# Output projection of a decoder layer in seven half-block products, residual and last bias by accumulating DMAs

## The chip, the core and the metric

The kernel runs on one core of one Trainium2 chip. The metric is the device time in microseconds of one execution, the median of three runs. The core has a matrix engine (TensorE, PE in the profile), VectorE (DVE), ScalarE (ACT), GpSimd (POOL) and SyncE (SP), each with its own instruction stream. SP and POOL issue the DMAs, each into its own queue. The engines meet only through semaphores.

## What is computed

One layer over 2048 tokens and 1024 channels, in float32. The part that the change touches is the last two lines: the output projection, the gated residual and the LayerNorm.

```python
h = x * (1.0 + scale) + shift
proj = h @ w_in[layer] + b_in[layer]
...
merged = jax.nn.sigmoid(g_mix_a) * y_attn + jax.nn.sigmoid(g_mix_b) * y_conv
sub = gate * (merged @ w_out[layer] + b_out[layer])
x = _layer_norm(DEEPNORM_ALPHA * x + sub, ln_g[layer], ln_b[layer])
```

The LayerNorm takes mean and variance over the 1024 channels of each token, then multiplies by `ln_g` and adds `ln_b`.

## The kernel before

Every large product is made in three passes of a rounded type: each operand is split into a high part (ScalarE copies it into the rounded type) and a low part (VectorE subtracts the high part from the original). The passes are high by high, high by low and low by high. So one product of a 128 x 512 result over 128 channels costs three matmuls of 512 columns.

**Input projection (68 groups).** A group computes a 2 x 2 block of results, two tiles of 128 outputs by two halves of 512 tokens, over two halves of the channels. It does this with seven products in place of eight (`NP = 7`): `combine` makes the sums and differences of the weight blocks on VectorE, `round_w` (ScalarE) and `split_w` (VectorE) make high and low parts, `product` issues 12 matmuls. The products are numbered n = 7 * group + p, and all five engines run the same loop over m, this number: ScalarE rounds the weights of product m + 4, VectorE splits those of m + 3 and takes the results of product m - 1, TensorE runs product n once its parts are there and its PSUM bank is free. Product p = 6 starts only when VectorE has taken p = 4 of its group (`pe.wait_ge(c22_out, g + 1)`).

**SP's queue in that loop.** `load_w(g)` fetches the weights of a group. `load_mix(u, dg)` fetches attention results, in nine DMAs for a unit u. The first unit is loaded at m = 448 to 450 and consumed by VectorE's `mix` at m = 452, 453, 454 (`MIX_AT`), after the taking and splitting of the same step. SP runs ahead of the other engines and stands only at its semaphore waits, so all nine DMAs leave right behind `load_w(65)`.

**Attention and conv projections (32 units n).** `project_att(n)` and `project_conv(n)` make a 128 x 512 tile. `gate_att` and `merge` on VectorE weigh both with their gates, and POOL's `store_m` writes the merged tile to `mix_d`. The gate-weighted output weights lie in `wos_d` since the middle of the kernel. During the last eight units SP loads them (`load_wo`), ScalarE rounds and VectorE splits them.

**Output projection (16 tiles tt of 128 tokens).** `load_m` fetches the merged rows of a tile, `round_m` and `split_m` make its parts, and TensorE runs 2 halves x 8 channel blocks x 3 passes = 48 matmuls for each tile, with the tokens as the stationary operand. `load_xr` fetches the residual rows. VectorE makes alpha * x + gate * bias, adds the product, takes mean and variance with `bn_stats`, and after ScalarE's normalization multiplies by `ln_g` and adds `ln_b`. POOL stores the tile. The last tile (`LAST`) is added and measured in two halves and stored in two halves.

## Time and profile before

| | us |
|---|---|
| median of 3 runs | 1870.26 (1868.84 to 1872.65) |
| the profiled execution, own time | 1868.47 |
| its span in the trace | 1866.7 |
| TensorE busy in the span | 1849.8 |
| VectorE busy | 1214.1 |
| ScalarE busy | 840.7 |

The page gives for each engine its busy time, its share of the span and its number of instructions. In a timeline each row is a start, a duration, an engine, a line, the operation with its tiles, a count, and in brackets how long the engine stood before it and for whom. DMA rows give the size of one and the median time from issue to landing. A matmul row's duration overlaps the next one's, so the pace is read from starts.

### The profile page before, as it was taken

How to read it: one execution, taken by the hardware profiler on the slowest of the kernel's cores; microseconds unless marked ns; L12 is line 12 of the kernel's file. 1: busy time of each engine (PE TensorE's matmuls, PEld its weight loads, DVE VectorE, ACT ScalarE, POOL GpSimd, SP SyncE). 2: the span in 40 equal slices, each digit the busy share in tenths (PEclk: the TensorE clock that was granted, in tenths of full speed). 3: DMA queues.
4: the chain of work that ended last, by engine and by line, in shares of the span. 5: the costliest groups of instructions: out<-in, count | busy, mean ns of one | idle time of the engine just before them, and what ended most of it. 6: DMA issues, size and time to landing. Idle time of an engine off the chain costs nothing.

```text
span 1866.7 us, 24546 instructions
## 1 busy us (share of the span) xinstructions
PE 1849.8 (99%) x8879; PEld 1508.0 (81%) x8879; DVE 1214.1 (65%) x2086; ACT 840.7 (45%) x1493; POOL 183.0 (10%) x305
## 2 busy tenths in 40 slices
PE   8999999999999999999999999999999999999998
PEld 7788888888888888878878888888888888888886
DVE  8755744456666666675686766666657576646776
ACT  5644633445545555666674545555454310012221
POOL 0223011100000000111210000000111100000000
PEclk9999999999999999999999999999999999999999
DMA  9866523332322222455853222222354988784442
GB/s 372 296 234 242 200 111 113 98 128 72 111 88 95 86 95 82 153 190 180 296 212 101 94 80 91 82 88 87 113 176 135 287 238 225 219 276 135 147 136 101
DMA packets 156648, 292.38 MB, mean 157 GB/s; under 512 B 35344, under 2 KB 87312, under 8 KB 152816
## 3 DMA queue, kind: packets, MB, share of 16 engines
q1 hardware_dynamic: 131056, 202.87, 33.9%
q0 software_dynamic: 25184, 87.35, 12.7%
q8 instruction: 72, 1.18, 0.3%
q10 hardware_dynamic: 288, 0.59, 0.1%
q14 instruction: 48, 0.39, 0.1%
HBM read 202.37 MB, written 88.38 MB: 156 GB/s over the span
## 4 chain that ended last, share of the span: by engine, by line
PE 95%; DVE 2%; ACT 1%; DMA 1%; issue 1%; ACTq 0%; POOL 0%; DVEq 0%
PE acc L1120 22%; PE acc L1125 21%; PE acc L1128 21%; PE acc L1329 3%; PE acc L1278 3%; PE acc L1282 3%; PE acc L1321 3%; PE acc L1325 3%; PE acc L1274 3%; PE score L1185 2%; PE xb L1218 2%; PE acc L1136 1%; PE xb L1201 1%; PE pt_o L1201 1%; DMA vt_d<-room 1%
## 5 line engine op out<-in xcount | busy, mean ns | idle before, releaser
L1120 PE MATMUL acc<-t_hi,w_hi 128*128 128x512 f32 x1848 | 509.2, 397 | 3.0 <-DVE room L1625 1.8
L1125 PE MATMUL acc<-t_lo,w_hi 128*128 128x512 f32 x1848 | 495.0, 390 | 0.0
L1128 PE MATMUL acc<-t_hi,w_lo 128*128 128x512 f32 x1848 | 494.9, 390 | 0.0
L1125 PEld LDWEIGHTS acc<-t_lo,w_hi 128*128 128x128 f32 x1848 | 346.9, 188 | 74.1
L1128 PEld LDWEIGHTS acc<-t_hi,w_lo 128*128 128x128 f32 x1848 | 346.9, 188 | 73.8
L1120 PEld LDWEIGHTS acc<-t_hi,w_hi 128*128 128x128 f32 x1848 | 337.1, 188 | 82.2 <-issue 13.1
L1625 DVE TENSOR_TENSOR room<-acc,part 128x512 f32<-128x512 f32 x198 | 136.8, 691 | 219.7 <-PE acc L1128 213.9
L1421 ACT ACTIVATE part<-acc,cols 128x512 f32<-128x512 f32 x198 | 136.8, 691 | 209.8 <-PE acc L1128 209.4
L1625 DVE TENSOR_TENSOR room<-room 128x512 f32<-128x512 f32 (+3 forms) x223 | 176.5, 795 | 73.8 <-ACT room L1451 30.7
L1625 DVE TENSOR_TENSOR w_lo<-w_raw,w_hi 128x512 fp32r<-128x512 f32 x272 | 183.7, 687 | 40.8 <-ACT w_hi L1404 39.2
L1404 ACT CAST w_hi<-w_raw 128x512 fp32r<-128x512 f32 x264 | 162.8, 617 | 90.2 <-PE acc L1128 87.6
L1404 ACT CAST w_hi<-s_tmp 128x512 fp32r<-128x512 f32 x198 | 122.9, 621 | 164.5 <-PE acc L1128 147.3
L1625 DVE TENSOR_TENSOR w_lo<-s_tmp,w_hi 128x512 fp32r<-128x512 f32 x198 | 136.2, 688 | 69.2 <-ACT w_hi L1404 66.5
L1486 ACT ACTIVATE room<-room 128x128 f32<-128x128 f32 (+1 forms) x192 | 86.9, 454 | 54.7 <-DVE room L1871 54.5
L1001 POOL DMA_DIRECT2D att_d<-room x48 | 34.5, 718 | 530.1 <-DVE room L1878 530.1
L1625 DVE TENSOR_TENSOR w_raw<-w_raw 128x512 f32<-128x512 f32 x98 | 67.5, 689 | 4.9
L1867 DVE CUSTOM_DVE_ANT_0 room<-score,room 128x128 f32<-128x128 f32 (+1 forms) x192 | 58.7, 362 | 16.6 <-PE score L1185 16.3
L1625 DVE TENSOR_TENSOR w_raw<-acc,w_raw 128x512 f32<-128x512 f32 x32 | 22.1, 690 | 68.1 <-PE acc L1282 68.1
L1625 DVE TENSOR_TENSOR s_tmp<-w_raw,s_tmp 128x512 f32<-128x512 f32 x66 | 45.6, 690 | 29.4 <-PE acc L1128 26.3
L1505 ACT CAST t_hi<-t_raw 128x2048 fp32r<-128x2048 f32 x6 | 11.5, 1917 | 116.6 <-DMA t_raw<-conv_d 116.6
L1321 PE MATMUL acc<-t_hi 128*128 128x512 f32 x256 | 63.2, 389 | 0.0
L1329 PE MATMUL acc<-t_hi,t_lo 128*128 128x512 f32 x256 | 63.2, 389 | 0.0
(224 smaller groups left out, 2067.8 us busy)
## 6 DMA issues: line engine op xcount, KB each, us to landing
w_raw<-in_w_tiles SPq DMA_DIRECT2D x132, 512.0 KB, 4.5
gate_d<-room POOLq DMA_DIRECT2D x64, 256.0 KB, 3.8
w_raw<-gate_d SPq DMA_DIRECT2D x32, 512.0 KB, 5.6
qk_d<-room POOLq DMA_DIRECT2D x24, 512.0 KB, 5.1
room<-qk_d SPq DMA_DIRECT2D x74, 128.0 KB, 3.6
t_raw<-tr_d SPq DMA_DIRECT2D x8, 1024.0 KB, 7.1
conv_d<-room POOLq DMA_DIRECT2D x16, 512.0 KB, 3.0
mix_d<-w_raw POOLq DMA_DIRECT2D x32, 256.0 KB, 5.6
```

The lines of the kernel that those rows point to most:

```text
L1120: nc.tensor.matmul(to, w_hi[:, s, k], t_hi[:, p, k], start=(first and k == 0), stop=False, skip_group_check=True)
L1125: nc.tensor.matmul(to, w_hi[:, s, k], t_lo[:, p, k], start=False, stop=False, skip_group_check=True)
L1128: mm = nc.tensor.matmul(to, w_lo[:, s, k], t_hi[:, p, k], start=False, stop=(last and k == KH - 1), skip_group_check=True)
L1274: nc.tensor.matmul(to, w_h[:, k], b_half(True, k), start=(k == 0), stop=False)
L1278: nc.tensor.matmul(to, w_l[:, k], b_half(True, k), start=False, stop=False)
L1321: nc.tensor.matmul(to, m_h[:, k], wo_hi[:, k, w], start=(k == 0), stop=False)
L1329: mm = nc.tensor.matmul(to, m_l[:, k], wo_hi[:, k, w], start=False, stop=(k == KT - 1))
L1404: nc.scalar.copy(w_hi[:, n % RING], src).then_inc(hi_done, 1)
L1421: ins = nc.scalar.activation(to, src, ACT.Identity, bias=col(gr.tb if p == 1 else gr.ta))
L1486: ex = nc.scalar.activation(prob[:, h, o], prob[:, h, o], ACT.Exp, bias=all_m[:, t, h, b], scale=SCALE, accum_out=all_d[:, t, h, b])
L1625: return nc.vector.tensor_tensor(o, a, b, op)
L1867: own_t.up(nc.vector.tensor_tensor_reduce(out=prob[:, h, o], in0=sc_ps[:, h, o], in1=bm[:, h, o.start - 2 * P * s:2 * P], scale=1.0, scala ...
```

## The change

The output projection gets the seven-product scheme of the input projection. Its 16 tiles become 8 blocks (`NO`) of 256 tokens. A block is two token tiles by two halves of 512 outputs over two halves of the channels. The loop numbers go on past the 476 products of the input projection (`NS`) to 532 (`NALL`). `product`, `round_w`, `split_w` and `combine` serve both: the stationary operand is the merged tokens, which `load_m(h)` now puts into `w_raw`, and the moving one is the output weights.

- Three of the four combinations of the output weights and one block more come from a new DRAM tensor `to_d`. It is made during the input projection in four rounds (`WQ_AT` = 425, 431, 437, 443): SP loads 1 MB of `wos_d`, VectorE makes four differences, POOL stores 1 MB.
- `load_to`, `round_to` and `split_to` bring in the seven weight blocks. Four of them are prepared on VectorE in the last eight units, three in the first steps of the output stage.
- The residual: ScalarE scales x by alpha (`scale_x`), and POOL adds the row gate * bias to it with an accumulating DMA (`residual`), read from DRAM 128 times over. `take_y` on VectorE adds the seven products to it, and sums the rows in the same instruction on the last four.
- The variance: ScalarE squares the centered row with a sum (`deviation`). VectorE centers and multiplies by `ln_g` (`center`), ScalarE scales (`scale_row`).
- The last bias: SP copies `ln_b` 1920 times into the output rows during the input projection (m = 446), DRAM to DRAM. POOL then adds each finished tile to the rows with an accumulating DMA (`shift_row`). The last tile keeps the old way.
- The gates and merged tiles of the last eight units lie in a place of their own (`mg_last`), since `w_raw` is needed for the tokens.

```diff
+NO = NTT // 2
+NALL = NS + NO * NP
+NX = 6
+WQ_AT = [ATT_END + 4 + 6 * r for r in range(KH)]
+M0 = NMU - KT
...
+    b_rows = ln_b.broadcast_to([LAST * P, D])
+    gb_rows = gb_d.broadcast_to([P, D])
...
+                def load_wq(r):
...
+                    sp.wait_ge(wq_out, 16 * r)
+                    src = wos_d.rearrange("(a k) p n -> k p a n", k=KH)[r]
+                    sp.dma_start(wq.rearrange("p (a b) n -> p a (b n)", a=2), src).then_inc(wq_in, 16)
...
+                def load_to(p):
+                    sp.wait_ge(mc_done, M0 + (0, 2, 4, 6, 8, 8, 8)[p])
...
+                    sp.dma_start(to_raw(p), src).then_inc(t_in[p % 4], 16)
...
+                    if m in WQ_AT:
+                        load_wq(WQ_AT.index(m))
+                    if m == WQ_AT[-1] + 3:
+                        sp.dma_start(out2[0:LAST * P, :], b_rows).then_inc(b_filled, 16)
...
+                load_to(4)
+                load_to(5)
+                load_to(6)
...
+                def residual(tt):
+                    pool.wait_ge(x_scaled, tt + 1)
+                    if tt >= 4:
+                        pool.wait_ge(r_taken, 2 * (tt // 2) - 2)
+                    pool.dma_start(xs[tt % NX], gb_rows, accum_op=ALU.add).then_inc(r_in[tt // 2 % 2], 16)
+
+                def shift_row(tt):
+                    pool.wait_ge(normed, tt + 1)
+                    pool.dma_start(out2[tt * P:(tt + 1) * P, :], xs[tt % NX], accum_op=ALU.add).then_inc(outs[tt // 2 % 3], 16)
...
+                residual(0)
+                residual(1)
+                pool.wait_ge(b_filled, 16)
+                for h in range(NO):
+                    if h < NO - 1:
+                        residual(2 * h + 2)
+                        residual(2 * h + 3)
+                    shift_row(2 * h)
+                    if h < NO - 1:
+                        shift_row(2 * h + 1)
...
-                for tt in range(NTT):
-                    r = tt % 2
-                    pe.wait_ge(m_hi_done, tt + 1)
...
+                for n in range(NS, NALL):
+                    product(n)
...
+                def deviation(tt):
+                    r = tt % 2
...
+                    act.wait_ge(nmu_ready, tt + 1)
+                    nc.scalar.activation(squares, xs[tt % NX], ACT.Square, bias=nmu[:, r:r + 1],
+                                         accum_out=ssq[:, r:r + 1]).then_inc(squared, 1)
...
+                for m in range(NS, NALL + 2):
+                    if m + 4 < NALL:
+                        round_w(m + 4)
+                    if m < NS + 3:
+                        round_to(m - NS + 4)
+                    h, p = (m - NS) // NP, (m - NS) % NP
+                    if p == 3 and h < NO - 1:
+                        scale_x(2 * h + 2)
+                        scale_x(2 * h + 3)
+                    if p == 6:
+                        deviation(2 * h)
+                    if p == 0 and h:
+                        deviation(2 * h - 1)
+                        scale_row(2 * h - 2)
+                    if p == 1 and h and 2 * h - 1 < LAST:
+                        scale_row(2 * h - 1)
...
+                def take_y(n):
+                    g, p = at(n)
...
+                    dve.wait_ge(prod, n + 1)
+                    if first is None:
+                        dve.wait_ge(r_in[tt // 2 % 2], 32 * (tt // 4 + 1))
+                    else:
+                        dve.wait_ge(first, g - 1)
+                    if p < 3 or tt == LAST:
+                        tt_op(y, bank(g, p), y, ALU.add).then_inc(done, 1)
...
+                for m in range(NS, NALL + 1):
+                    if m > NS:
+                        take_y(m - 1)
+                    h, p = (m - NS) // NP, (m - NS) % NP
+                    if p == 0 and h:
+                        center(2 * h - 2)
+                    if p == 1 and h:
+                        center(2 * h - 1)
+                    for n, when in enumerate((-4, -3, -2, 0)):
+                        if (m - when) % NP == 0 and NG + (when < 0) <= (m - when) // NP < NG + NO:
+                            combine((m - when) // NP, n)
+                    if m + 3 < NALL:
+                        split_w(m + 3)
+                    if NS < m <= NS + 3:
+                        split_to(m - NS + 3)
+                finish_last()
```

SP's queue late in the input projection. `in_w_tiles` is `load_w`, `att_d`, `wg_d` and `za_d` are the nine DMAs of `load_mix` for the first unit. Before:

```order
L628 DMA w_raw<-in_w_tiles 128x1024 [waits lo_done]
L628 DMA w_raw<-in_w_tiles 128x1024
L776 DMA room<-att_d 128x4x128 [waits att_out1,att_out0,wg_out]
L779 DMA room<-wg_d 64x512 x2
L783 DMA room<-za_d 128x512 [waits za_out]
```

Now, with the last two loads of `wos_d` ahead of the weights:

```order
L867 DMA room<-wos_d 128x2x1024 [waits wq_out] x2
L664 DMA w_raw<-in_w_tiles 128x1024 [waits lo_done]
L664 DMA w_raw<-in_w_tiles 128x1024
L936 DMA out_x<-in_ln_b 1920x1024
L812 DMA room<-att_d 128x4x128 [waits att_out1,att_out0,wg_out]
L815 DMA room<-wg_d 64x512 x2
L819 DMA room<-za_d 128x512 [waits za_out]
```

The copy of 1920 rows stands between the weights of group 65 and the nine loads.

VectorE at the start of the output stage, right after the last `merge`. `t_lo<-t_raw` and `w_lo<-wl_raw` of 2048 are `split_to`, those of 512 are `split_w`, `acc` is a product's result. Now:

```order
L1739 TENSOR_TENSOR room<-acc,room 128x512 [waits r_in0,prod]
L1739 TENSOR_TENSOR w_lo<-w_raw,w_hi 128x512 [waits hi_done]
L1739 TENSOR_TENSOR t_lo<-t_raw,t_hi 128x2048 [waits t_hi_done]
L1739 TENSOR_TENSOR part<-acc,part 128x512 [waits r_in0,prod]
L1739 TENSOR_TENSOR t_lo<-s_tmp,t_hi 128x512 [waits hi_done]
L1739 TENSOR_TENSOR t_lo<-t_raw,t_hi 128x2048 [waits t_hi_done]
L1739 TENSOR_TENSOR room<-acc,room 128x512 [waits r_in0,prod]
```

Before, all parts of the output weights stood ahead of the first tile, and a tile was taken in one instruction. Now two of the large splits stand between the takings of the first three products.

VectorE at the end. Before, from the last half's sum:

```order
L1625 TENSOR_TENSOR room<-acc,room 128x512 [waits y_done]
L2141 BN_STATS stats<-room 128x6 [waits vector_own]
L2143 BN_AGGR mv<-stats 128x2 [waits vector_own]
L2148 SCALAR_TENSOR_TENSOR room<-room,mv 128x512 [waits var_ready]
L2152 RECIPROCAL rstd<-std 128x1 [waits std_ready]
```

Now:

```order
L1739 TENSOR_TENSOR room<-acc,room 128x512 [waits r_in1,prod]
L2128 BN_STATS stats<-room 128x6 [waits c21_dve]
L2137 BN_AGGR mv<-stats 128x2 [waits vector_own]
L2147 RECIPROCAL rstd<-std 128x1 [waits normed,std_ready]
L2152 SCALAR_TENSOR_TENSOR room<-room,nmu 128x1024 [waits vector_own,nmu_ready]
L2160 SCALAR_TENSOR_TENSOR room<-room,mv 128x512 [waits var_ready]
```

The centering of the tile before the last one has come between the last tile's variance and its first half.

## Rows read from the trace of the kernel before

**Rows 1.** The page: busy time, share, instructions; then the chain that ended last

```profile
PE 1849.8 (99%) x8879; PEld 1508.0 (81%) x8879; DVE 1214.1 (65%) x2086; ACT 840.7 (45%) x1493; POOL 183.0 (10%) x305
...
PE 95%; DVE 2%; ACT 1%; DMA 1%; issue 1%; ACTq 0%; POOL 0%; DVEq 0%
```

**Rows 2.** Timeline of PE: products of the input projection, then first and last output tile

```profile
1402.24 1.07 PE L1120 MATMUL acc<-t_hi,w_hi 128*128 128x512 f32 x4
...
1404.96 1.07 PE L1120 MATMUL acc<-t_hi,w_hi 128*128 128x512 f32 x4
...
1407.68 1.07 PE L1120 MATMUL acc<-t_hi,w_hi 128*128 128x512 f32 x4
...
1685.12 1.98 PE L1321 MATMUL acc<-t_hi 128*128 128x512 f32 x8
...
1848.32 1.98 PE L1321 MATMUL acc<-t_hi 128*128 128x512 f32 x8
```

**Rows 3.** Timeline of SP around the first unit of `load_mix`

```profile
1379.91 0.80 SPq L628 DMA_DIRECT2D w_raw<-in_w_tiles  x2
1380.82 0.38 SPq L776 DMA_DIRECT2D room<-att_d  x1
...
1385.40 7.07 SPq L779 DMA_DIRECT2D room<-wg_d  x2
```

**Rows 4.** Timeline of DVE: around the `wos` rounds, then where `mix` stands

```profile
1370.98 0.69 DVE L1625 TENSOR_TENSOR w_lo<-s_tmp,w_hi 128x512 fp32r<-128x512 f32 x1 [0.50 <-DVE room L1625]
...
1404.48 0.69 DVE L1625 TENSOR_TENSOR room<-room 128x512 f32<-128x512 f32 x1
1405.21 0.69 DVE L1625 TENSOR_TENSOR room<-acc,part 128x512 f32<-128x512 f32 x1
...
1410.56 2.56 DVE L1625 TENSOR_TENSOR room<-room 128x512 f32<-128x512 f32 x3
...
1414.91 1.29 DVE L1625 TENSOR_TENSOR w_lo<-w_raw,w_hi 128x512 fp32r<-128x512 f32 x2
```

**Rows 5.** Stretches: busy times of five engines, granted clock, DMA share, GB/s

```profile
10.00:20.00 10.00, 7.12 (x25) 5.39 (x24) 10.00 (x15) 6.26 (x7) 0.00 (x0) 0.83 1.03 411
20.00:30.00 10.00, 10.00 (x46) 8.28 (x45) 10.00 (x17) 6.03 (x7) 0.00 (x0) 1.00 1.02 400
```

**Rows 6.** DMA issues of the first 45 us: KB each, median us to landing

```profile
room<-in_x_t SPq DMA_DIRECT2D x8, 512.0 KB, 13.5
...
tr_d<-room POOLq DMA_DIRECT2D x1, 1024.0 KB, 4.9
```

**Rows 7.** DMA issues of the whole span

```profile
room<-in_x SPq DMA_DIRECT2D x16, 512.0 KB, 3.7
...
out_x<-room POOLq DMA_DIRECT2D x14, 512.0 KB, 2.9
...
t_raw<-wos_d SPq DMA_DIRECT2D x4, 1024.0 KB, 8.1
...
out_x<-room SPq DMA_DIRECT2D x2, 256.0 KB, 2.0
```

**Rows 8.** Groups by line and form: count, busy us, mean ns, idle before

```profile
L1625 DVE TENSOR_TENSOR t_lo<-t_raw,t_hi 128x2048 fp32r<-128x2048 f32 x19 | 43.5, 2287 | 3.1 <-ACT t_hi L1409 2.8
...
L2124 DVE SCALAR_TENSOR_TENSOR room<-room 128x1024 f32<-128x1024 f32 x16 | 19.5, 1218 | 0.5 <-DVE room L1625 0.5
```

**Rows 9.** Groups of ACT: the rounding of an output weight block, the normalization

```profile
L1614 ACT ACTIVATE room<-room,nmr,rstd 128x1024 f32<-128x1024 f32 x15 | 18.7, 1247 | 6.4 <-DVE nmr L2160 6.4
...
L1513 ACT CAST t_hi<-t_raw 128x2048 fp32r<-128x2048 f32 x4 | 7.7, 1916 | 68.5 <-DMA t_raw<-wos_d 68.5
```

**Rows 10.** Timeline: the last `merge`, then the last tile from its last sum

```profile
1685.32 0.69 DVE L1625 TENSOR_TENSOR w_raw<-acc,w_raw 128x512 f32<-128x512 f32 x1 [0.21 <-PE acc L1282]
...
1859.39 0.69 DVE L1625 TENSOR_TENSOR room<-acc,room 128x512 f32<-128x512 f32 x1 [0.80 <-PE acc L1329]
...
1863.40 0.75 DVE L2154 SCALAR_TENSOR_TENSOR room<-room,rstd 128x512 f32<-128x512 f32 x1
```

More of the change, by code:

```diff
@@ L378, in build @@
         mod_ready = sem("mod_ready")
-        x_in = [sem(f"x_in{r}") for r in range(4)]
+        x_in = [sem(f"x_in{r}") for r in range(2)]
         h_ready = sem("h_ready")
@@ new lines, in wait_m_last, with load_m @@
+                def wait_m_last():
+                    for r in range(3):
+                        sp.wait_ge(m_last[r], 16 * len(range(r, KT, 3)))
+                def load_m(h):
+                    for r in range(2):
+                        sp.wait_ge(m_out[r], 16 * M0 // 2)
+                    if h >= 6:
+                        wait_m_last()
+                    if h >= 2:
+                        sp.wait_ge(lo_done, NP * (NG + h - 1))
+                    for n in range(2):
+                        tok = slice((2 * h + n) * P, (2 * h + n + 1) * P)
+                        to = w_raw[:, h % 2, 2 * n:2 * n + 2].rearrange("p b k n -> p (b k) n")
+                        sp.dma_start(to, mix_d[:, :, tok].rearrange("k p n -> p k n")).then_inc(raw_in[h % 2], 16)
@@ L910, in _ @@
+                load_to(6)
+                sp.wait_ge(gb_ready, 1)
+                sp.wait_ge(ya_done, NMU)
+                for to, src in ((g_bc, ln_g), (b_bc, ln_b)):
+                    sp.dma_start(to, src.broadcast_to([P, D])).then_inc(bc_in, 16)
+                load_x(1)
+                load_x(2)
+                for h in range(2, NO):
+                    load_m(h)
+                    if h >= 3:
+                        load_x(h)
                 for half in range(2):
-                    sp.wait_ge(affine, LAST + half + 1)
+                    sp.wait_ge(last_affine, half + 1)
@@ L918, in _ @@
+                sp.wait_ge(last_out, 32)
             @block.gpsimd
@@ new lines, in center @@
+                def center(tt):
+                    r = tt % 2
+                    dve.wait_ge(std_ready, tt + 1)
+                    if tt >= 2:
+                        dve.wait_ge(normed, tt - 1)
+                    own_t.up(nc.vector.reciprocal(rstd[:, r:r + 1], std[:, r:r + 1]))
+                    if tt < 2:
+                        dve.wait_ge(bc_in, 64)
+                    dve.wait_ge(nmu_ready, tt + 1)
+                    own_t.wait()
+                    nc.vector.scalar_tensor_tensor(out=xs[tt % NX], in0=xs[tt % NX], scalar=nmu[:, r:r + 1], in1=g_bc,
+                                                   op0=ALU.add, op1=ALU.mult).then_inc(centered, 1)
@@ new lines, in finish_last @@
+                def finish_last():
+                    y, r = xs[LAST % NX], LAST % 2
+                    dve.wait_ge(var_ready, 1)
+                    for half in range(2):
+                        o = slice(half * CH, (half + 1) * CH)
+                        own_t.up(nc.vector.scalar_tensor_tensor(out=y[:, o], in0=y[:, o], scalar=mv[:, 0:1], in1=g_bc[:, o],
+                                                                op0=ALU.subtract, op1=ALU.mult))
+                        if half == 0:
+                            dve.wait_ge(std_ready, LAST + 1)
+                            own_t.up(nc.vector.reciprocal(rstd[:, r:r + 1], std[:, r:r + 1]))
+                        own_t.wait()
+                        nc.vector.scalar_tensor_tensor(out=y[:, o], in0=y[:, o], scalar=rstd[:, r:r + 1], in1=b_bc[:, o],
+                                                       op0=ALU.mult, op1=ALU.add).then_inc(last_affine, 1)
```

383 lines of the change are left out of this document (195 added, 188 removed).

## Prediction, made before the result was known

> **What bounds the kernel now.** I read the page's busy times first: TensorE is busy 1849.8 of 1866.7 us, and the chain that ended last is PE for 95% [rows 1]. So time is gained only by fewer matmuls, and lost wherever another engine or a DMA lets TensorE stand. Then the timeline, for the pace. In the input projection the first matmuls of three products start at 1402.24, 1404.96 and 1407.68: 2.72 us for 12 matmuls, 0.2267 each. In the output stage 15 tiles of 48 matmuls take 1848.32 - 1685.12 = 163.20 us, 0.2267 each as well [rows 2]. The output stage runs at full pace without a gap, and there is nothing in it to win but the matmuls themselves.
>
> **Fewer products.** 16 tiles x 48 = 768 matmuls before, 8 blocks x 7 products x 12 = 672 now. 96 x 0.2267 = **21.8 us less**. The pace of the new form is that of the input projection, shown above. The combinations are on VectorE. For a block of 256 tokens it now has 7 takings, 4 combinations and 7 splits of 0.69 us, some 0.1 us more where a sum goes along, 2 centerings of 1.22 and some small ones, about 16 us of 19.04 us (7 x 2.72) for seven products. ScalarE has 7 roundings of 0.62 and 6 passes over a row of 1.25 us [rows 9], some 12.5 us. Both fit, and by the order three products of parts lie ready, so I cost the steady stage at nothing beyond the matmuls.
>
> **The seam between the stages.** Before, the last `merge` ran under the first output tile [rows 10] and nothing waited. Now four things meet from 1685.1 on. The last three weight blocks, 1 MB each, leave only when the last unit is done. One such load took 8.1 us to land (median, little behind it) [rows 7], I take 7.4, 11.4 and 15.4 us for the three, 4 us apart since other transfers share the engines. Each is rounded in 1.92 us [rows 9] and split in 2.29 us [rows 8]. POOL can issue the first two residual DMAs only after the last merged tile is stored, about 3 us into the stage. Plain ones of that size land in 2.9 to 3.7 us [rows 7]. For the pair of accumulating ones I take 6, so the first product, done at 2.7, is taken at 9.6. Product 2 wants it taken at 5.4: 4.2 us lost. VectorE then goes through split, split of block 4 (to 12.6), taking, split, split of block 5 (to 16.3), taking of product 2 (17.0). Product 4, which could start at 15.1, waits for that: 2 us. Block 6 and the taking of product 4 cost another 1.3. Sum **7.5 us**. Bounds: 2 us, if the accumulates land like plain stores and the loads in 6 us, and 13, if the pair takes 12 us.
>
> **The tail.** Before, from the last sum at 1859.39 to the end of the span are 7.3 us, and the last row instruction ends at 1864.15 [rows 10]. Now the centering of tile 14, 1.22 [rows 8] + 0.16 us, stands ahead of the last tile on VectorE. Its scaling by ScalarE (1.25) ends 4.5 us after the last product. Its accumulating store is issued at about 5, and lands some 5 us later: end at 10.0 us. **2.7 us more**, bounds 1.4 (the centering alone) and 6.
>
> **The rounds for the combined weights.** Each round puts 4 x 0.69 = 2.8 us on VectorE and 2 MB on the queues. No taking of a product stands right behind three of them, and parts are three products ahead, so no price. But the third store (behind VectorE's sums, which end about 1374.5 [rows 4], landing 4.9 us for 1 MB [rows 6]) holds SP till about 1381.5, the fourth load goes ahead of the weights of group 65, and what follows finds 2 MB ahead of it: at 400 GB/s till about **1386**.
>
> **The copy of 1920 rows.** This is the term on which the sign rests. It is 1920 x 4 KB = 7.86 MB on SP's own queue, right ahead of the nine loads of the first `load_mix` (the order in the section on the change). Before, these leave at 1380.82 [rows 3], right behind the weights, and VectorE uses the first at 1404.48 without a wait [rows 4]. That a load waits for what is ahead in its queue shows at the start of the kernel: 512 KB land in 13.5 us there, against 3.7 in the output stage [rows 6, 7]. How fast does it run? The trace has no transfer from DRAM to DRAM. Lower bound: the rate of loads, 400 to 411 GB/s [rows 5], gives 19.5 us. Upper: a read and a write one after the other. Stores run at 786 KB in 4.9 - 2.0 = 2.9 us, 271 GB/s [rows 6, 7], so 19.5 + 29 = 48.5 us. I take 39 us, every byte counted twice against the rate of loads, since both sides are in the same memory. So the copy ends at 1386 + 39 = 1425, and the first loads land at 1427.
>
> What queues behind the wait: VectorE stands at `mix` (m = 452) with the taking of product 452 behind it, done at 1427 + 0.7 + 0.8 = 1428.5. Product 454 needs that taking, and started at 1407.68 [rows 2]: 20.8 us. The last of the nine loads leaves SP till 1392.47, 11.65 us after the first [rows 3]. So it lands at 1438.7. Behind the third part of `mix` (2.6 + 0.5 + 0.7 us) stand a combination and a split, done at 1443.8. Product 458 wants that split in its last third, 1428.5 + 4 x 2.72 + 1.8 = 1441.2: 2.6 us. Together **23.4 us**. After such a gap TensorE has lost its clock: in the stretch 10 to 20 us, after it had stood, the granted clock is 0.83 [rows 5], the lower level for a part of it, 10 x 0.17 = **1.7 us**.
>
> By the lower bound the same arithmetic gives 1.2 + 2.7 = 3.9 us and no clock. By the upper one 32.9.
>
> The Trainium skill has two figures that bear on this. "DMA: Bandwidth & Descriptors", section Bandwidth, gives 425 GB/s for 16 MB from HBM to SBUF, and its section "Latency and other measured facts" gives 214 GB/s for copies between HBM tensors. By the one the copy would take 18.5 us and the sum below would be -8.7 us, by the other 36.7 us and +11.2. The first agrees with rows 5. No run here has yet shown the second.
>
> **Sum.** -21.8 + 7.5 + 2.7 + 23.4 + 1.7 = **+13.5 us**. Against the profiled execution's own time, 1868.5, that is 1882.0. The median of the runs is 1.8 above that execution, so 1883.8.
>
> **Rivals.**
> - *The copy is fast.* Reads and writes overlap in the DMA engines, and it takes about 20 us. For it: the engines moved 411 GB/s at the start [rows 5]. Against it: stores alone gave 271. Sum -21.8 + 7.5 + 2.7 + 3.9 = -7.7, so 1862.6, and 1857 where the seam costs 2. This is the faster side. It holds till the copy takes 22 us. From 22 to 29 us (270 to 357 GB/s) the gain and the wait cancel within 3.7 us, 0.2%. So a rate of about 310 GB/s is break-even.
> - *Accumulating DMAs are slow* (the slower side, in another place). In a block of 19.04 us POOL issues four of 512 KB, 4.76 us each if the queue is to keep up. Plain stores need (2.9 - 2.0) x 2 = 1.8 us of transfer [rows 7], and reading the target as well doubles it to 3.6, so it should fit. If one needs 6 us, each of seven blocks takes 24 us: 35 us more, 1918 with the forecast's copy and 1897 with the fast one. VectorE would wait in `take_y` for the residual. This decides from 4.76 us for one on.
>
> **How the numbers follow.** Copy above 29 us: 0.48. Copy of 22 to 29 us: 0.12. Fast copy: 0.26. Slow accumulates: 0.14. The likeliest is the first, 1883.8, its own range 1877 to 1894 (copy of 33 to 48.5 us, seam 2 to 13). The range from 1858 to 1897 takes in the fast copy with most of its seam, and leaves out the slow accumulates with the slow copy and the extremes. Faster by over 0.2% (about what a measurement of this kernel can tell from no change) 0.26, within it 0.12, slower 0.62.
>
> **What the new profile would show.** 96 fewer matmuls at 0.2267 us. The landing time of the copy, 39 us. VectorE waiting some 20 us in one piece for `att_d` or `wg_d` at about 1405 and TensorE behind it. Three short waits of TensorE in the first six products of the output stage, for the takings of products 0, 2 and 4. A landing of 4 to 5 us for the accumulates, and no wait for them from the second block on. About 10 us from the last sum to the end. The forecast is wrong if the copy lands in under 29 us, or if loads overtake it in the queue.

## The result, and the profile of the changed kernel

| | before | changed |
|---|---|---|
| median of the runs, us | 1870.97 (1868.84 to 1872.65) | 1904.15 (1903.26 to 1908.09) |
| ratio, 95% interval | | 1.0184 (1.0168 to 1.0200) |
| profiled execution, span, us | 1866.7 | 1901.8 |
| matmuls | 8879 | 8783 |
| granted clock, mean | 0.999 | 0.984 |

The changed kernel is 33.2 us slower. The forecast had the sign, but 1883.8 us, and its range ended at 1897. All 96 matmuls are gone, and TensorE is busy for a smaller share of a longer span. Beside [rows 1], the page's busy times and chain of the changed kernel:

```profile
PE 1831.9 (96%) x8783; PEld 1492.7 (78%) x8783; DVE 1223.4 (64%) x2170; ACT 891.4 (47%) x1582; POOL 206.0 (11%) x327
...
PE 85%; DMA 6%; SPq 3%; DVE 3%; issue 1%; ACT 1%; POOL 0%; ACTq 0%; DVEq 0%
```

The chain has lost ten points of PE and gained DMA and SyncE's queue. Where, shows in the timeline of PE. It answers to [rows 2]: first the place of the copy, then the first products of the output stage.

```profile
1409.36 1.07 PE L1237 MATMUL acc<-t_hi,w_lo 128*128 128x512 f32 x4
1437.60 2.05 PE L1229 MATMUL acc<-t_hi,w_hi 128*128 128x512 f32 x4 [27.16 <-DVE room L1739]
...
1721.81 1.07 PE L1237 MATMUL acc<-t_hi,t_lo 128*128 128x512 f32 x4
1738.25 2.04 PE L1229 MATMUL acc<-t_hi 128*128 128x512 f32 x4 [15.37 <-DVE room L1739]
```

There are two gaps, 27.16 and 15.37 us. Behind each the same four matmuls take 2.05 instead of 1.07 us: TensorE is at its lower level, 1.2 GHz, for most of one product (granted clock 0.50 from 1437.6 to 1441.5 us and from 1738.0 to 1742.5 us), which costs 2.2 us the first time and 2.1 the second. In everything else the pace is that of before, 2.72 us for a product.

**First gap: the copy.** Timeline of SP, against [rows 3]:

```profile
1385.29 0.79 SPq L936 DMA_DIRECT2D out_x<-in_ln_b  x1
1386.20 19.06 SPq L812 DMA_DIRECT2D room<-att_d  x1
1405.30 10.80 SPq L815 DMA_DIRECT2D room<-wg_d  x2
```

The DMA issues of the stretch from 1380 to 1445 us (KB each, median us from issue to landing):

```profile
out_x<-in_ln_b SPq DMA_DIRECT2D x1, 7680.0 KB, 47.8
...
gate_d<-room POOLq DMA_DIRECT2D x7, 256.0 KB, 9.3
...
to_d<-room POOLq DMA_DIRECT2D x1, 1024.0 KB, 13.8
room<-att_d SPq DMA_DIRECT2D x3, 256.0 KB, 19.4
room<-wg_d SPq DMA_DIRECT2D x6, 128.0 KB, 13.2
```

The copy takes 47.8 us, 7.86 MB read and 7.86 MB written. SyncE is held too: the one issue behind the copy stands 19.06 us. Timeline of DVE at the same place, where [rows 4] shows no wait, and then at the third product of the output stage:

```profile
1413.16 0.69 DVE L1739 TENSOR_TENSOR room<-acc,part 128x512 f32<-128x512 f32 x1 [11.65 <-DMA gate_d<-room]
...
1436.03 0.69 DVE L1739 TENSOR_TENSOR room<-room 128x512 f32<-128x512 f32 x1 [20.74 <-DMA room<-wg_d]
...
1737.41 0.69 DVE L1739 TENSOR_TENSOR room<-acc,room 128x512 f32<-128x512 f32 x1 [12.62 <-DMA part<-gb_d]
```

The loads of the mix hold VectorE 20.74 us, as forecast. Before that it stands 11.65 us for the landing of a gate store, which is in GpSimd's queue, not in SyncE's. This first wait adds nothing to the gap of TensorE here: the taking that TensorE waits for stands behind the mix, and that is held by the later wait in any case.

**Second gap: the seam.** The stage starts at 1717.28. Timeline of DVE behind that:

```profile
1719.22 2.29 DVE L1739 TENSOR_TENSOR t_lo<-t_raw,t_hi 128x2048 fp32r<-128x2048 f32 x1 [2.84 <-ACT t_hi L1602]
...
1722.03 0.69 DVE L1739 TENSOR_TENSOR room<-acc,room 128x512 f32<-128x512 f32 x1
```

Timeline of POOL:

```profile
1723.73 0.54 POOL L1117 DMA_DIRECT2D mix_d<-room  x1 [7.12 <-DVE room L1739]
1724.27 0.94 POOL L1163 DMA_DIRECT2D room<-gb_d  x1
1724.85 1.27 POOL L1163 DMA_DIRECT2D part<-gb_d  x1
```

The landings of this pair, from the DMA issues of 1710 to 1745 us:

```profile
room<-gb_d POOLq DMA_DIRECT2D x1, 512.0 KB, 10.1
part<-gb_d POOLq DMA_DIRECT2D x1, 512.0 KB, 12.5
```

The last unit's merge stands on VectorE behind the split of the fourth weight block (the first row above). That split waits 2.84 us for ScalarE's rounding, and ScalarE had stood 4.63 us for the block's load. So the unit's store and, behind that, the residual pair leave GpSimd 7 us into the stage. The pair then takes 10.1 and 12.5 us to land.

**The tail.** From the last sum (1887.46) to the span's end are 14.3 us, where [rows 10] had 7.3. The last issue of GpSimd, by the timeline:

```profile
1892.02 0.85 POOL L1167 DMA_DIRECT2D out_x<-room  x1 [15.51 <-ACT room L1624]
```

SP's waits in the last 50 us (us in total, times, longest):

```profile
SPq L995 <- DMA out_x<-room: 4.1, 1, 4.1
SPq L657 <- PEq L657: 3.4, 1, 3.4
```

The engines' draining at the block's end (ns least, median and most, then first and last start):

```profile
L657 POOLq DRAIN  x1: 9578/9578/9578, 1892.0 to 1892.0; - x1
...
L657 SPq DRAIN  x1: 7/7/7, 1898.3 to 1898.3; - x1
```

All data are stored at 1898.2, but the span ends at 1901.8. The wait is named after PEq, yet the row that lasts that long is GpSimd's: its drain runs 9.58 us from its last issue, to 1901.6. In the kernel before, GpSimd issued nothing after tile 13, and its drain lay under the last tile:

```profile
L621 POOLq DRAIN  x1: 7739/7739/7739, 1846.5 to 1846.5; - x1
```

**The sum of the spans.** -21.8 (matmuls) + 27.2 + 2.2 (copy) + 15.4 + 2.1 (seam) + 7.0 (tail) = +32.1. The spans differ by 35.1. A further 2.6 us are there before the copy, most of it in the first 100 us. Busy time of PE in the first 100 us of the kernel before (stretch, PE busy, clock, DMA share, GB/s):

```profile
0.00:100.00 100.00, 93.35 (x395) 0.98 0.90 333
```

The same in the run e3_before_plus_copy below, which is the same code up to 1380 us:

```profile
0.00:100.00 100.00, 91.46 (x384) 0.97 0.87 327
```

So 1.9 us of the 2.6 do not come from the change. The profiled execution of before ran 2.5 us under its median, and the run e7_all below, which has the change, shows 93.11.

### The profile page after: what moved, and what is told of

Read it like the earlier page. It is cut to its first block, busy times and chain, and to the rows that moved or that the text cites. A ratio compares the mean times of both kernels' runs of the same rounds, so it can differ in the third digit from the quotient of the medians.

```text
span 1901.8 us, 24773 instructions
## 1 busy us (share of the span) xinstructions
PE 1831.9 (96%) x8783; PEld 1492.7 (78%) x8783; DVE 1223.4 (64%) x2170; ACT 891.4 (47%) x1582; POOL 206.0 (11%) x327
## 4 chain that ended last, share of the span: by engine, by line
PE 85%; DMA 6%; SPq 3%; DVE 3%; issue 1%; ACT 1%; POOL 0%; ACTq 0%; DVEq 0%
PE acc L1229 23%; PE acc L1234 22%; PE acc L1237 22%; PE acc L1387 2%; PE acc L1391 2%; PE acc L1383 2%; PE score L1294 2%; PE xb L1327 2%; DMA room<-wg_d 1%; PE acc L1245 1%; DVE room L1739 1%; SPq L812 1%; PE xb L1310 1%; PE pt_o L1310 1%; DMA vt_d<-room 1%
## 5 line engine op out<-in xcount | busy, mean ns | idle before, releaser
L1229 PE MATMUL acc<-t_hi,w_hi 128*128 128x512 f32 x1888 | 520.6, 397 | 30.8 <-DVE room L1739 29.6
L1234 PE MATMUL acc<-t_lo,w_hi 128*128 128x512 f32 x1888 | 506.7, 390 | 0.0
L1237 PE MATMUL acc<-t_hi,w_lo 128*128 128x512 f32 x1888 | 505.8, 390 | 0.0
L1229 PEld LDWEIGHTS acc<-t_hi,w_hi 128*128 128x128 f32 x1888 | 345.0, 188 | 111.8 <-issue 40.9
L1234 PEld LDWEIGHTS acc<-t_lo,w_hi 128*128 128x128 f32 x1888 | 355.0, 188 | 76.0
L1237 PEld LDWEIGHTS acc<-t_hi,w_lo 128*128 128x128 f32 x1888 | 354.9, 188 | 75.1
L1739 DVE TENSOR_TENSOR room<-room 128x512 f32<-128x512 f32 (+3 forms) x217 | 156.3, 724 | 86.7 <-ACT room L1540 30.6
L1739 DVE TENSOR_TENSOR s_tmp<-w_raw,s_tmp 128x512 f32<-128x512 f32 x74 | 51.0, 689 | 27.3 <-PE acc L1237 24.3
L1739 DVE TENSOR_TENSOR t_lo<-t_raw,t_hi 128x2048 fp32r<-128x2048 f32 (+1 forms) x29 | 57.6, 1992 | 14.6 <-ACT t_hi L1602 11.0
L1102 POOL DMA_DIRECT2D gate_d<-room x64 | 34.9, 547 | 270.8 <-ACT room L1526 270.7
L1229 PE MATMUL acc<-t_hi 128*128 128x512 f32 x152 | 41.6, 396 | 15.4 <-DVE room L1739 15.4
```

Of the source, the lines that this page charges most:

```text
L1229: nc.tensor.matmul(to, hi_w[:, k], hi_t[:, k], start=(first and k == 0), stop=False, skip_group_check=True)
L1234: nc.tensor.matmul(to, hi_w[:, k], lo_t[:, k], start=False, stop=False, skip_group_check=True)
L1237: mm = nc.tensor.matmul(to, lo_w[:, k], hi_t[:, k], start=False, stop=(last and k == KH - 1), skip_group_check=True)
L1739: return nc.vector.tensor_tensor(o, a, b, op)
```

## The experiments

All times are medians beside runs of the kernel before on the same chip. Its median was 1869.62 us beside e1 to e4, 1870.13 beside e5 to e8 and 1870.25 beside e9 and e10.

### Where the copy is issued

```diff
-                    if m == WQ_AT[-1] + 3:
-                        sp.dma_start(out2[0:LAST * P, :], b_rows).then_inc(b_filled, 16)
...
+                    if m == WQ_AT[-1] + 3:
+                        act.dma_start(out2[0:LAST * P, :], b_rows).then_inc(b_filled, 16)
```

> The changed kernel with one edit: the 7.86 MB copy of the last bias into the output is issued on ScalarE's queue at the same step (446) instead of on SyncE's. All data, sizes and the moment of issue stay. Theory Q (queue order): the nine loads of the mix stand behind the copy in SyncE's queue and begin only when it has ended; in another queue they share the DMA engines with it, so gate_d and wg_d land after some 5 to 10 us, the two waits of VectorE (11.65 and 20.74 us) fall to under 10 us together, the gap of TensorE of 27.16 us falls to under 8 us, and the time is about 1882 us. Theory B (bandwidth): the 47.8 us are taken from the DMA engines whoever issues them; the gap stays at 20 us or more and the time within 4 us of 1904.

Measured 1902.59 us, ratio 1.0173 (1.0156 to 1.0190): as slow as the changed kernel. The landing of the copy:

```profile
out_x<-in_ln_b ACTq DMA_DIRECT2D x1, 7680.0 KB, 53.1
```

The two gaps, by the timeline of PE:

```profile
1417.93 2.05 PE L1227 MATMUL acc<-t_hi,w_hi 128*128 128x512 f32 x4 [6.11 <-DVE room L1739]
...
1449.03 2.07 PE L1235 MATMUL acc<-t_hi,w_lo 128*128 128x512 f32 x4 [15.87 <-DVE w_lo L1739]
```

The gap is split in two, 6.11 and 15.87 us, and each has a product at the lower clock behind it. Theory Q falls for the time, and was half right for the mechanism. Of the loads of the mix, which leave SyncE from 1386.0 on (ScalarE issues the copy at 1390.2), two `att_d` land in 7.2 us at most, `za_d` in 7.9 and the median `wg_d` in 8.9. But the third `att_d` takes 47.4 us and the slowest `wg_d` 48.2. VectorE waits 11.43 and 21.63 us, as before. The moment of issue did not stay as it was: ScalarE comes to its step 4.9 us later than SyncE did (1390.20 against 1385.29 us), and the loads that landed early are those that SyncE had issued by then. The third `att_d`, issued at 1390.81 us, is the first one behind the copy. So this run shows that loads behind the copy in time land late though they are in another queue, and loads ahead of it do not. Why the engines let the copy go first stays open. The gate store's wait, which was covered before, makes the first gap here.

### The copy in pieces

```diff
+FILL_AT = [at for at in TWO_AT if at >= 319][:LAST]
...
-                    if m == WQ_AT[-1] + 3:
-                        sp.dma_start(out2[0:LAST * P, :], b_rows).then_inc(b_filled, 16)
+                    if m in FILL_AT:
+                        k = FILL_AT.index(m)
+                        sp.dma_start(out2[k * P:(k + 1) * P, :], b_rows[k * P:(k + 1) * P, :]).then_inc(b_filled, 16)
```

> The changed kernel with the same 7.86 MB copy cut into fifteen pieces of 128 rows (512 KB), one at each of fifteen steps from step 319 on, where SyncE's queue has room between the weight loads, instead of one piece ahead of the mix loads. Both theories on the copy expect the gap of 27.16 us and the cold product behind it (2.2 us) to go: 1904.15 - 29.4 = 1874.8 us, and the products' start of the output stage back from 1717.3 to about 1688. The rival 'there is no spare bandwidth anywhere' expects the pieces (about 2.5 us each at 411 GB/s for read and write) to come back as waits of TensorE on weights in the stage from 1000 to 1300 us: then 1885 to 1904 us.

Measured 1873.48 us, ratio 1.0023 (1.0013 to 1.0033): 30 us of the 33 are gone, against 29.4 expected. The pieces, issued from 1003 to 1261 us, by the DMA issues:

```profile
out_x<-in_ln_b SPq DMA_DIRECT2D x15, 512.0 KB, 5.8
```

The seam, by the timeline of PE:

```profile
1708.13 2.04 PE L1231 MATMUL acc<-t_hi 128*128 128x512 f32 x4 [16.16 <-DVE room L1741]
```

A piece lands in 5.8 us. TensorE waits 1.3 us in all from 900 to 1300 us, exactly as in the kernel before. The same bytes cost 29 us in one place and nothing in another. The gap of the seam stays (16.16 us), so it does not come from the copy. The next kernels start from this one, where it is not said otherwise.

### The copy alone

```diff
+                    if m == 446:
+                        sp.dma_start(fill_d, ln_b.broadcast_to([LAST * P, D])).then_inc(b_filled, 16)
```

> The kernel before with one part of the change alone: the 7.86 MB copy of the last bias, issued by SyncE at step 446 in front of the mix loads, here into a scratch tensor that nobody reads; the output projection stays as it was. If the copy alone makes the 29.4 us: 1870.97 + 29.4 = 1900.4 us, with a gap of TensorE of about 27 us near 1405 to 1435 us. If half of the gap came from the other new traffic there (the combined weights, the longer waits of the gate stores), the gap is 10 to 18 us and the time 1883 to 1890 us.

Measured 1893.96 us, ratio 1.0132 (1.0116 to 1.0147), 24.3 us more than before, and between the two expectations. The landing:

```profile
fill_d<-in_ln_b SPq DMA_DIRECT2D x1, 7680.0 KB, 44.9
```

The gap of PE:

```profile
1432.15 2.05 PE L1125 MATMUL acc<-t_hi,w_hi 128*128 128x512 f32 x4 [21.48 <-DVE room L1630]
```

The copy alone makes a gap of 21.48 us. The traces of the two runs divide the other 5.7 us of the changed kernel's gap. There the copy lands 2.9 us later after its issue (47.8 against 44.9). It is issued 25.2 us before TensorE stops instead of 27.1 (1385.29 and 1383.59 us, with the gaps beginning at 1410.44 and 1410.67), 1.9 us less. And TensorE starts 4.5 us after the landing instead of 3.7.

### The combined weights out of the copy's way

From the changed kernel, the copy still at step 446 (`FILL_AT`):

```diff
-WQ_AT = [ATT_END + 4 + 6 * r for r in range(KH)]
+WQ_AT = [ATT_END + 2 + 5 * r for r in range(KH)]
+FILL_AT = ATT_END + 4 + 6 * (KH - 1) + 3
...
-                    if m == WQ_AT[-1] + 3:
+                    if m == FILL_AT:
```

> The changed kernel with one size edit: the four rounds of the combined weights run at steps 423, 428, 433 and 438 instead of 425, 431, 437 and 443, so that their last 1 MB store is issued some 5 steps earlier (about 1383 us instead of 1394.4 us) and is out of the way before the 7.86 MB copy, which stays at step 446. The kernel before with the copy alone had a gap of 21.5 us where the changed kernel has 27.2 us. Theory W (the difference is that store, 1 MB read and 1 MB written beside the copy, about 5 us of all DMA engines at 411 GB/s): the gap falls to 21 to 23 us and the time to about 1899 us. Rival (the difference is of another kind, as the earlier start of the output stage's other transfers, or chance): gap 26 to 28 us, time within 2 us of 1904.

Measured 1910.25 us, ratio 1.0211 (1.0196 to 1.0227): slower, by 6 us. Neither theory had that. The gaps of PE:

```profile
1359.97 2.05 PE L1230 MATMUL acc<-t_hi,w_hi 128*128 128x512 f32 x4 [9.94 <-DVE room L1740]
...
1444.28 2.04 PE L1230 MATMUL acc<-t_hi,w_hi 128*128 128x512 f32 x4 [24.45 <-DVE room L1740]
```

The gap at the copy falls by 2.7 of the 5.7 us (27.16 to 24.45), and the copy lands in 45.2 us. But a new gap of 9.94 us opens at 1360: VectorE stands 9.59 us for `room<-wos_d`. The timeline of SP shows where that load was:

```profile
1336.64 13.45 SPq L786 DMA_DIRECT2D room<-stat_d  x24
1350.13 0.55 SPq L868 DMA_DIRECT2D room<-wos_d  x1
```

The second round's load stands in SyncE's queue behind 24 small loads of `stat_d`, which take the queue 13.45 us. In the changed kernel it stands behind the same 24 and leaves at 1353.26 us, but there VectorE's sums come three steps later and wait only 3.80 us for it, without a gap of TensorE. So the new gap comes from this place in the queue. At the copy, the landing is 2.6 us shorter (45.2 us, close to the 44.9 of the copy alone), since the last 1 MB store was issued 3.8 us ahead of the copy and not 9.2 us behind it. That agrees with theory W for about half of the 5.7 us. The new gap ahead of it moved the other transfers too, so this run does not separate the store from them.

### How the gap grows with the copy

From the changed kernel, with 8 of the 15 parts at step 446 and seven spread:

```diff
+FILL_AT = [at for at in TWO_AT if at >= 319][:LAST - 8]
...
                     if m == WQ_AT[-1] + 3:
-                        sp.dma_start(out2[0:LAST * P, :], b_rows).then_inc(b_filled, 16)
+                        sp.dma_start(out2[0:8 * P, :], b_rows[0:8 * P, :]).then_inc(b_filled, 16)
+                    if m in FILL_AT:
+                        k = 8 + FILL_AT.index(m)
+                        sp.dma_start(out2[k * P:(k + 1) * P, :], b_rows[k * P:(k + 1) * P, :]).then_inc(b_filled, 16)
```

> The changed kernel with the copy cut in two sizes: eight of its fifteen parts (4.19 MB) stay in one piece at step 446, the other seven go one by one at seven steps from step 319 on, where they cost nothing. If the engines share their time and the wait grows one for one with the bytes, the piece lands after 47.8 x 8/15 = 25.5 us, 22.3 us sooner, the gap falls from 27.2 to about 5 us and the time to about 1880 us. If the wait is in proportion to the size (no part of the copy is hidden), the gap is 27.2 x 8/15 = 14.5 us and the time about 1890 us.

Measured 1882.21 us, ratio 1.0058 (1.0041 to 1.0075). The landing of the larger part:

```profile
out_x<-in_ln_b SPq DMA_DIRECT2D x1, 4096.0 KB, 28.6
```

The gap of PE:

```profile
1417.16 2.04 PE L1233 MATMUL acc<-t_hi,w_hi 128*128 128x512 f32 x4 [7.77 <-DVE room L1743]
```

The landing is 19.2 us shorter (47.8 to 28.6) and the gap 19.4 us shorter (27.16 to 7.77). One for one, as the first expectation said. In both sizes the gap is the landing less some 20.7 us, which are hidden. But the wait behind it is another one now, by the timeline of DVE:

```profile
1411.99 0.69 DVE L1743 TENSOR_TENSOR room<-acc,part 128x512 f32<-128x512 f32 x1 [11.51 <-DMA gate_d<-room]
```

The mix loads hold VectorE only 1.48 us more after it. The gate store's wait is as long as in the changed kernel and makes most of this gap, as it makes the 6.11 us of e1. What a still smaller piece would cost here is not shown.

### What the addition in the DMAs costs

```diff
-                    pool.dma_start(xs[tt % NX], gb_rows, accum_op=ALU.add).then_inc(r_in[tt // 2 % 2], 16)
+                    pool.dma_start(xs[tt % NX], gb_rows).then_inc(r_in[tt // 2 % 2], 16)
...
-                    pool.dma_start(out2[tt * P:(tt + 1) * P, :], xs[tt % NX], accum_op=ALU.add).then_inc(outs[tt // 2 % 3], 16)
+                    pool.dma_start(out2[tt * P:(tt + 1) * P, :], xs[tt % NX]).then_inc(outs[tt // 2 % 3], 16)
```

> The kernel with the copy in fifteen pieces, and the two accumulating DMAs of each output tile turned into plain ones of the same size, queue and moment. What is left out: the residual row is overwritten by the bias row instead of added to it, and the last bias is not added; all instructions and waits stay. Theory A (the accumulation itself is what is slow): the first pair lands in 3 to 5 us instead of 10.1 and 12.5, the seam's gap of 15.37 us falls to about 5, the last tile's store takes 3 to 4 us instead of 9.8; together 14 to 17 us less than with the copy in pieces alone, about 1859 us. Theory L (load: 3 MB of weight blocks are in flight beside the pair): the landing stays over 8 us, the gap over 11 us, only the tail shortens by some 3 to 6 us: about 1870 us.

Measured 1869.82 us, ratio 1.0000 (0.9991 to 1.0010), 3.7 us less than with the additions. The gap of the seam, by the timeline of PE:

```profile
1705.39 2.05 PE L1231 MATMUL acc<-t_hi 128*128 128x512 f32 x4 [11.74 <-DVE room L1741]
```

The steady stage, 1760 to 1840 us (PE busy, clock, DMA share, GB/s), with the additions (e2_copy_spread):

```profile
1760.00:1840.00 80.00, 80.00 (x355) 1.00 0.94 212
```

and without:

```profile
1760.00:1840.00 80.00, 80.00 (x355) 1.00 0.53 190
```

Theory L holds for the seam: the pair lands in 8.0 and 8.8 us instead of 10.1 and 13.2, and of 16.16 us of gap the additions make 4.4. The rest is load and the late issue. The steady stage is not touched, but it is nearer to its limit than it looks. The additions raise the DMA share from 0.53 to 0.94. That is 0.41 x 19.04 / 4 = 1.95 us of all engines for each of the four per block, and it leaves 0.06 x 19.04 = 1.1 us free in a block. The tail did not shorten by 3 us, though the last store lands 1.9 us sooner (3.4 against 5.3). The 9.8 us that I had expected of that store in the changed kernel were the time from its issue to the end of the span; its landing was 5.4. That led to GpSimd's drain, for which the wait in the page's words points at PEq.

### The first pair on VectorE

The edit of VectorE; GpSimd's `residual(0)`, `residual(1)` and ScalarE's two scalings go:

```diff
+                    if n == M0 + 7:
+                        dve.wait_ge(x_in[0], 32)
+                        dve.wait_ge(gb_ready, 1)
+                        for tt in range(2):
+                            nc.vector.scalar_tensor_tensor(out=xs[tt], in0=xs[tt], scalar=ALPHA, in1=gb,
+                                                           op0=ALU.mult, op1=ALU.add).then_inc(x_scaled, 1)
```

> The kernel with the copy in fifteen pieces, and one part of the change undone at one place: the residual of the first pair of tiles (0 and 1) is made by VectorE (two products and sums of 128x1024 just before the split of the fourth weight block, where it idles 2.86 us for ScalarE) instead of by ScalarE's two scalings and two accumulating DMAs. The other seven pairs keep their DMAs. Theory: the gap of 16.16 us of TensorE in front of the third product is the landing of that pair (13.2 us) and nothing else, since VectorE would have stood ready 13.4 us earlier; the gap falls to about 3 us, and the time from 1873.5 to about 1860 us. Rival (the weight blocks are next): rounding and splitting of blocks 3 to 6 is late by nearly as much, and the gap comes back in smaller ones in front of the products 3 to 6: a gain of 4 to 8 us only, 1866 to 1870 us.

Measured 1862.17 us, ratio 0.9959 (0.9946 to 0.9973). Timeline of PE:

```profile
1696.03 1.35 PE L1229 MATMUL acc<-t_hi 128*128 128x512 f32 x4 [3.00 <-DVE room L1736]
...
1718.46 1.16 PE L1229 MATMUL acc<-t_hi,w_hi 128*128 128x512 f32 x4 [1.39 <-DVE room L1736]
```

The gap falls from 16.16 to 3.00 us, as the theory said. The clock still falls behind it (granted clock 0.57 from 1696.5 to 1699.0 us), and the first product takes 4.4 us instead of 2.72. By the ratios 12.0 us are gained of the 13.5 expected. A gap of 1.39 us appears at the second pair, whose DMAs are the first to be waited for now (VectorE stands 1.25 us for `room<-gb_d`). The weight blocks do not take the seam's place.

### The first pair by DMA, but earlier

```diff
                 for n in range(NMU):
+                    if n == NMU - 1:
+                        residual(0)
+                        residual(1)
                     store_m(n)
```

and ScalarE's two scalings ahead of its rounding of the fourth block.

> The kernel with the copy in fifteen pieces, and the first pair's residual still by ScalarE and accumulating DMAs, but earlier: scaled ahead of ScalarE's work for the fourth weight block, and issued on GpSimd's queue ahead of the last store of the mix instead of behind it, so at about 1685.5 us instead of 1693.4 us. Theory O (order of issue): the pair lands at 1694 to 1699 us instead of 1707.2, the gap of 16.16 us falls to 2 to 7 us, the time to 1860 to 1866 us. Theory L (the three weight blocks and the two rows of 4 MB in all hold the DMA engines until about 1700 us whoever comes first): it lands after 1701 us, the gap stays over 9 us, the time is 1867 us or more.

Measured 1865.68 us, ratio 0.9978 (0.9968 to 0.9987). Timeline of POOL:

```profile
1684.98 0.95 POOL L1165 DMA_DIRECT2D room<-gb_d  x1
1685.78 1.05 POOL L1165 DMA_DIRECT2D part<-gb_d  x1
```

and of PE:

```profile
1697.07 1.24 PE L1232 MATMUL acc<-t_hi 128*128 128x512 f32 x4 [3.42 <-DVE room L1742]
```

Theory O holds: the pair lands at 1696.2, and the gap is 3.42 us. With the same DMAs, 12.7 of the 16.2 us of the gap go by order alone. Counted from the start of the output stage (1688.05 us here, 1686.37 in e2_copy_spread), the second DMA is issued 9.9 us earlier, and it lands in 10.4 instead of 13.2 us. The time falls by less, 8.4 us by the ratios: two more short waits of 0.35 and 1.07 us come behind, and this execution began the stage 1.7 us later. So it was the moment of issue, not the accumulating form, that made most of the seam.

### The tail without GpSimd

The edit of VectorE; SyncE then stores the tile as a whole, and GpSimd's last `shift_row` goes:

```diff
+                center(LAST - 1)
+                y, r = xs[(LAST - 1) % NX], (LAST - 1) % 2
+                dve.wait_ge(centered, LAST)
+                nc.vector.scalar_tensor_tensor(out=y, in0=y, scalar=rstd[:, r:r + 1], in1=b_bc,
+                                               op0=ALU.mult, op1=ALU.add).then_inc(last_affine, 1)
```

> The kernel with the copy in fifteen pieces, and one part of the change undone at the end: the last but one tile is finished by VectorE (scaled and shifted there) and stored by SyncE with a plain DMA, so that GpSimd issues no DMA after the last product. Theory: of the 14.2 us from the last product's end to the span's end, 9.4 us are GpSimd's draining of its queue after its last, accumulating store (from 1862.6 to 1872.1 us), which also outlasts that store's landing by 3.4 us; with the drain earlier the end comes after SyncE's last store, about 4 us sooner: 1869.5 us. Rival (the work on VectorE, 1.28 us more behind the last tile, and the 512 KB store take it back): 1872 to 1874 us.

Measured 1871.31 us, ratio 1.0008 (0.9998 to 1.0017), 2.8 us less than e2_copy_spread by the ratios. The two intervals overlap, so the trace has to carry this claim. SP's last wait:

```profile
SPq L658 <- PEq L658: 0.2, 1, 0.2
```

GpSimd's drain:

```profile
L658 POOLq DRAIN  x1: 9585/9585/9585, 1846.6 to 1846.6; - x1
```

From the last sum (1858.43) to the end (1869.1) are 10.7 us, 3.5 less than the 14.2 of e2_copy_spread. The drain takes as long (9.58 us), but starts at 1846.6, under the last products, and the last wait is 0.2 us again. The mechanism is the one expected, and 3.5 of the expected 4 us came.

### All three repairs

The edits of e2, e5 and e6 together:

> The changed kernel with three edits together: the copy in fifteen pieces, the first pair's residual on VectorE, and the last but one tile finished by VectorE and stored by SyncE. If the three stalls are independent, their gains add: 1904.15 - 30.7 (copy, as measured) - 13 (seam) - 4 (tail) = about 1856 us, 13 us under the kernel before, of whose 21.8 us of saved products some 8 are then still lost (a gap of about 3 us and colder products at the seam, 3 us of the tail, and the 512 KB issues). If the weight blocks take the seam's place: 1862 to 1866 us.

Measured 1858.15 us, ratio 0.9936 (0.9923 to 0.9948): 12.0 us faster than the kernel before, and 46 us faster than the changed one. The busy times on the page:

```profile
PE 1828.5 (98%) x8783; PEld 1489.5 (80%) x8783; DVE 1227.3 (66%) x2173; ACT 888.2 (48%) x1579; POOL 203.6 (11%) x324
```

What is left at the seam, by the timeline of PE:

```profile
1694.47 1.17 PE L1232 MATMUL acc<-t_hi 128*128 128x512 f32 x4 [2.42 <-DVE room L1740]
...
1701.27 1.16 PE L1232 MATMUL acc<-t_hi,w_hi 128*128 128x512 f32 x4 [1.08 <-DVE room L1740]
```

The gains add: -21.8 + 2.4 + 1.1 + 1.1 (three short gaps, the third at 1716.57) + 4.4 (tail of 11.7 instead of 7.3 us) = -12.8. Measured are -12.0 by the medians and -10.3 by the spans of the two profiled executions (1856.4 against 1866.7). Of the difference to the latter, 1.3 us lie ahead of the output stage, which starts at 1686.44 instead of 1685.12. So the seven-product form wins 12 of its 21.8 us here, and what made the changed kernel slower were transfers at three places: the copy, the first residual pair and the last store of GpSimd.

## Why the forecast was wrong

- **Fewer products, -21.8 us: right.** 96 fewer matmuls, at a pace of 2.72 us a product through the whole steady stage.
- **The copy, 23.4 + 1.7 us: mis-sized, 27.2 + 2.2 measured.** I took 39 us for its time, each byte counted twice against the rate of loads. It takes 44.9 us in the kernel before and 47.8 beside the store of the combined weights. That is 15.7 MB in 47.8 us, 329 GB/s counted twice, near my upper bound of 48.5. The Trainium skill ("DMA: Bandwidth & Descriptors", section "Latency and other measured facts") gives 214 GB/s for copies of 128 x 16 KiB tiles between HBM tensors, from which I had estimated 36.7 us. Measured were 7.86 / 44.9 = 175 GB/s in the kernel before and 164 in the changed one, for one repeated row and beside other traffic, so the measurement decides. The third part of the mix, 2.6 us in my sum, cost nothing.
- **Missed inside that term.** I asked only who stands behind the copy in SyncE's queue. The first to wait was VectorE's taking at 1413.16, for a gate store in GpSimd's queue. In the changed kernel the mix loads outlast that wait, as I had said, but it would leave a gap of some 6 us without them (6.11 in e1). With the copy on ScalarE's queue the time was the same. So "loads behind it in the queue" is not the whole cause: the copy fills the engines (DMA share 1.02 from 1400 to 1412 us), and what was issued behind it landed late in SyncE's and in GpSimd's queue.
- **Rounds for the combined weights, 0: wrong by the neighbour, not by themselves.** VectorE's sums cost nothing in place. By the traces, the gap exceeds that of the copy alone by 5.7 us, since the copy lands 2.9 us slower, is issued 1.9 us later against the products, and TensorE starts 0.9 us later after the landing. The first part fell to 0.3 us in e9, where the last 1 MB store was out of the way; why the other two changed is not shown.
- **The seam, 7.5 us (bounds 2 to 13): mis-sized, 17.5 measured, and outside the bounds.** Two numbers failed. I let the residual pair leave 3 us into the stage, and it left at 7 to 7.6, since the last merge stands behind the split of the fourth block on VectorE. And I took 6 us for its landing, which was 12.5. Together they put the end of the first taking at 20.8 us into the stage (1738.10 - 1717.28) instead of 9.6, so 4.2 + 11.2 = 15.4 us of gap, as measured. My upper bound had a landing of 12 us, but kept the early issue. The later waits of 3.3 us did not come (they were covered by the long one), and the 2.1 us of the lower clock did, a term that I had not in this sum.
- **The tail, 2.7 us (bounds 1.4 to 6): mis-sized, 7.0 measured.** The centering (1.3 us) was right. The landing of the accumulating store adds 2.5. The 3.2 us of GpSimd's drain I had not in my sum at all. The rows of before hide it, since the drain lies under the last tile there.
- **The rivals.** "The copy is fast" is out: it needed under 22 us. "Accumulating DMAs are slow in the steady stage" did not come true, but it was close. From 1.8 us for a plain transfer and 1.95 more for the addition, one takes some 3.75 us of the engines, against my 3.6. My break-even of 4.76 let the four DMAs have the engines to themselves. With the other loads of a block it was nearer: 1.1 us of 19.04 were left free in e2_copy_spread. The landings were 9.2 us for the residual rows and 5.5 for the output rows (medians of sixteen and fifteen), where I had named 4 to 5, and TensorE never waited for them after the first block.

Sum of the misses: copy 3.8 + 0.5, seam 10.0, tail 4.3 = 18.6 us. With the 2.6 us that were there before the copy these are 21.2 of the 21.6 us by which the difference of the spans (35.1) exceeds the forecast (13.5). So the seam, not the copy, was the largest error.

## What to carry to other kernels

A transfer of several megabytes that nobody waits for is cheap only where the DMA engines have spare time: at one place it cost 29 us, in pieces of 512 KB where the DMA share was 0.26 it cost nothing. Look at the share of the stretch, and at every store and load that lands there, in whatever queue. Where work moves from an engine to a DMA, the first use is the one to cost: ask when the issuing queue gets to it, and what else lands at that moment. And a DMA at the end of GpSimd's queue is paid with the drain, an accumulating one (3.4 us) as well as a plain one (4.6 us).

## What the runs showed of the hardware

- GpSimd's drain at the end of the block took 7.7 to 9.8 us from its last DMA issue: 7.7 and 8.8 us after a plain store, 9.4 to 9.8 after an accumulating one. As the last thing it outlasted the landing of all stores by 3.3 to 4.6 us. The profile names PEq as the releaser. Where SyncE's plain stores came last, its last wait was 0.2 us.
- Accumulating DMAs of 512 KB landed later than plain ones: 5.1 against 2.9 us to DRAM, 8.3 against 5.3 us for the residual rows (medians of 1740 to 1830 us, e2_copy_spread against e4_plain_dmas). They took 1.95 us more of all 16 engines each, worked out from the DMA shares.
- A DRAM to DRAM copy of 7.86 MB took 44.9 to 53.1 us, one of 4.19 MB 28.6 us, one of 512 KB 5.8 us, all beside other traffic. The issuing engine stood as well when such a copy was ahead: 19.06 us for one issue of SyncE.
